# First norm through four PSUM banks, group 0's heads in the prologue, and y rows between weight blocks in a hybrid decoder layer

## What is computed

```python
h = rms_norm(x, norm1_w[layer])
(q, k_c, v_c, k_s, v_s, k_w, v_w, g_nsa, z, xbc, dt_raw,
 gate_a, gate_b) = split_columns(h @ w_in[layer], IN_SIZES)
y_a = nsa_mixer(q, k_c, v_c, k_s, v_s, k_w, v_w, g_nsa, ...)
y_b = ssd_mixer(z, xbc, dt_raw, ...)
merged = jax.nn.sigmoid(gate_a) * (y_a @ w_proj_a[layer]) + jax.nn.sigmoid(gate_b) * (y_b @ w_proj_b[layer])
x = x + merged @ w_out[layer]
x = x + conv_glu_ffn(rms_norm(x, norm2_w[layer]), ffn_w_up[layer], ffn_conv_w[layer], ...)
```

## Time and profile before

| | us |
|---|---|
| three timed runs | 1333.57, 1332.92, 1329.69 (median 1332.92) |
| the profiled execution, whole | 1330.96 |
| its span, first to last instruction | 1329.2 |
| TensorE busy | 1274.7 (96%) |
| VectorE busy | 837.0 (63%) |
| ScalarE busy | 609.5 (46%) |
| DMA, mean rate over the span | 88 GB/s |

### The profile page before, as it was taken

How to read it: one execution, slowest core, us unless ns; L and a number is a source line. 1 busy time by engine, 2 the same in 40 slices (tenths; PEclk the granted TensorE clock), 3 DMA queues, 4 the chain that set the end, 5 groups by cost and what they waited for, 6 DMA issues and landing times.

```text
span 1329.2 us, 18048 instructions
## 1 busy us (share of the span) xinstructions
PE 1274.7 (96%) x6965; PEld 1080.2 (81%) x6965; DVE 837.0 (63%) x1571; ACT 609.5 (46%) x1080; POOL 66.8 (5%) x65
## 2 busy tenths in 40 slices
PE   3998999999999999999999989999999999999999
PEld 2797899879988899877987778887878888888887
DVE  3415788688968797778856443333487878775221
ACT  5524476657665576556664533222432222223110
POOL 1000000400012000400021000000000000000000
PEclk9999999999999999999999999999999999999999
DMA  7312222123221321132212823335223333334231
GB/s 241 102 48 64 64 52 69 41 52 92 57 56 46 98 57 48 41 96 57 64 40 80 284 81 94 95 95 174 64 81 94 95 95 95 95 95 127 95 127 48
DMA packets 185595, 116.37 MB, mean 88 GB/s; under 512 B 25918, under 2 KB 169638, under 8 KB 185510
## 3 DMA queue, kind: packets, MB, share of 16 engines
q1 hardware_dynamic: 182053, 108.92, 28.5%
q10 hardware_dynamic: 3456, 6.29, 1.2%
HBM read 106.80 MB, written 8.39 MB: 87 GB/s over the span
## 4 chain that ended last, share of the span: by engine, by line
PE 78%; DVE 12%; ACT 4%; DMA 2%; issue 2%; SPq 1%; ACTq 1%; DVEq 0%
PE g L556 13%; PE g L557 13%; PE g L558 13%; PE t L549 4%; PE g L589 3%; PE g L591 3%; PE g L590 3%; PE s L809 2%; PE s L714 2%; PE ob L730 2%; DVE w_low L1451 2%; PE s L895 2%; PE s L897 2%; PE s L896 2%; PE t L633 1%
## 5 line engine op out<-in xcount | busy, mean ns | idle before, releaser
L964 ACT ACTIVATE w_high<-wraw 128x1024 fp32r<-128x1024 f32 x175 | 185.1, 1058 | 301.5 <-DMA wraw<-in_ffn_w_up 143.3
L1451 DVE TENSOR_TENSOR w_low<-wraw,w_high 128x1024 fp32r<-128x1024 f32 x175 | 216.7, 1240 | 118.2 <-ACT w_high L964 111.6
L556 PE MATMUL g<-hT_hi,w_high 128*128 128x512 f32 x360 | 161.7, 449 | 5.6 <-DVE hT_lo L1458 3.9
L589 PE MATMUL g<-w_high,hT_hi 128*128 128x256 f32 x512 | 151.4, 296 | 0.0
L591 PE MATMUL g<-w_high,hT_lo 128*128 128x256 f32 x512 | 144.1, 281 | 0.0
L590 PE MATMUL g<-w_low,hT_hi 128*128 128x256 f32 x512 | 144.0, 281 | 0.0
L557 PE MATMUL g<-hT_lo,w_high 128*128 128x512 f32 x360 | 143.2, 398 | 0.0
L558 PE MATMUL g<-hT_hi,w_low 128*128 128x512 f32 x360 | 143.0, 397 | 0.0
L556 PE MATMUL g<-h2T_hi,w_high 128*128 128x512 f32 x352 | 139.9, 397 | 0.5 <-DVE w_low L1451 0.5
L557 PE MATMUL g<-h2T_lo,w_high 128*128 128x512 f32 x352 | 139.5, 396 | 0.0
L558 PE MATMUL g<-h2T_hi,w_low 128*128 128x512 f32 x352 | 139.5, 396 | 0.0
(11 more groups left out here) (319 smaller groups left out, 2515.6 us busy)
## 6 DMA issues: line engine op xcount, KB each, us to landing
wraw<-in_w_in SPq DMA_DIRECT2D x152, 256.0 KB, 3.3
wraw<-in_ffn_w_up SPq DMA_DIRECT2D x88, 256.0 KB, 3.2
wraw<-in_ffn_w_down SPq DMA_DIRECT2D x44, 256.0 KB, 3.1
wraw<-in_w_proj_b SPq DMA_DIRECT2D x32, 256.0 KB, 3.2
yT_lo<-spill SPq DMA_DIRECT2D x6, 1024.0 KB, 8.2
spill<-piece_e ACTq DMA_DIRECT2D x16, 256.0 KB, 3.5
wraw<-in_w_proj_a SPq DMA_DIRECT2D x16, 256.0 KB, 3.1
wraw<-in_w_out SPq DMA_DIRECT2D x16, 256.0 KB, 3.2
```

The costliest lines, as they stand in the source:

```text
L556: nc.tensor.matmul(gb[par][:, :], w, hi, start=k == 0, stop=False)
L589: nc.tensor.matmul(out_, hT[0][:, k, cols], w, start=k == 0, stop=False)
L964: nc.scalar.activation(whi[slot_of(u)][:, :, :], wraw[u % 2][:, :, :], ACT.Copy).then_inc(w_hi, 1)
L1451: V.tensor_tensor(wlo[slot_of(u)][:, :, :], wraw[u % 2][:, :, :], whi[slot_of(u)][:, :, :].bitcast(F32), ALU.subtract).then_inc(w_lo, 1)
```

## The change

Four edits that don't touch what is computed:

1. *Start.* The rows that the first norm needs (slot 2 of `prow`) are loaded from ScalarE's queue, and `pcol` slots 0 and 1 are transposed behind block 0. The root is taken in two pairs; row blocks 0 and 3 are scaled by VectorE, 1 and 2 by ScalarE. x goes through four banks (`s0`, `s1`, `s2`, `ob`) in place of two, first the pieces of row blocks 0 and 1 of four columns, then those of 2 and 3. ScalarE writes `hT_hi` only, and VectorE's difference reads the bank itself. Block 2 is loaded ahead of the compression weights, and SyncE no longer waits for the small loads.
2. *Group 0's heads.* `q_norm` and `k_norm` of group 0 stand ahead of `lo(13)`, their first two transposes at steps 6 and 7 of block 12. `bar[2]` goes. The biases, rounded values and last x evacuation of group 0 move behind block 12 and 13 on ScalarE.
3. *Groups.* SiLU of x ahead of the `pT_hi` of unit 7, SiLU of z right behind the last z evacuation, `qk_root` behind `p_low(7)`, `value_low` behind `ttr(0)` of the group it serves, the transposes of x one step earlier (3, 4, 5, 7 in place of 4, 5, 6, 7), `value_consts(0)` into unit 0.
4. *Gates.* The y transposes at step 7 of block 69 and steps 0 to 2 of block 70; one more gate block ahead of `bar[0]` for every engine; y parts 0 and 1 ahead of block 74's load, 2, 3 and 4 behind the loads of 74 to 76, part 5 between the first two merge blocks; the sigmoids of the early gates spread over three blocks; the merge waits for 2, 4 and 6 y parts in place of 6.

```diff
-            sp.wait_ge(p_loaded, 16 * 16)
+            halves(2, w_in_cols(C_KC + P))
             for q, name in enumerate(("cmp_wk1", "cmp_wv1")):
...
-            y_back(0)
-            for s in range(EARLY_GATES + 4, GATE_BLOCKS):
+            y_rows(0)
+            y_rows(1)
+            for s in range(EARLY_GATES + 5, GATE_BLOCKS):
                 gate_unit(s)
-                y_back(s - EARLY_GATES - 3)
-            y_back(5)
+                y_rows(s - EARLY_GATES - 3)
...
+            def start():
+
+                def columns(k, tiles=range(NT)):
+                    if k >= 4:
+                        pe.wait_ge(h_lo, k - 3)
+                    for i in tiles:
+                        last = nc.tensor.transpose(x1T_banks[k % 4][:, P * i:P * (i + 1)], xt[:, i, P * k:P * (k + 1)],
+                                                   ident[:, :])
+                    if NT - 1 in tiles:
+                        last.then_inc(xT_fill, 1)
+                for tiles in ((0, 1), (2, 3)):
+                    for i in tiles:
+                        pe.wait_ge(xn_ready[i], 1)
+                    for k in range(4):
+                        columns(k, tiles)
...
-            block_of(12)
-            pe.drain().then_inc(bar[2], 1)
+            block_of(12, {6: lambda: backs(0, 0), 7: lambda: backs(1, 0)})
...
+            def h_high(k):
+
+                act.wait_ge(xT_fill, k + 1)
+                nc.scalar.activation(hT[0][:, k, :], x1T_banks[k % 4][:, :], ACT.Copy,
+                                     scale=pcol[:, 2, N1 + k:N1 + k + 1]).then_inc(h_hi, 1)
...
+                    if n == 7:
+                        act.wait_ge(conv_done, g * 6 + 6)
+                        nc.scalar.activation(xcx[:, :, :], xcx[:, :, :], ACT.Silu).then_inc(xc_ready, 1)
...
+                early = {2: chan[:, :, :], 3: xraw[:, :, :], 4: sg[:, 0:2, :]}
+                if s - EARLY_GATES in early:
+                    part = early[s - EARLY_GATES]
+                    nc.scalar.activation(part, part, ACT.Sigmoid).then_inc(gates_ready, 1)
...
+            def h_rest(k):
+
+                dve.wait_ge(h_hi, k + 1)
+                V.scalar_tensor_tensor(hT[1][:, k, :], x1T_banks[k % 4][:, :], pcol[:, 2, N1 + k:N1 + k + 1],
+                                       hT[0][:, k, :].bitcast(F32), ALU.mult, ALU.subtract).then_inc(h_lo, 1)
...
-                    if n == 7 and g < G - 1:
-                        seq.fence()
-                        qk_root(g + 1)
                     lo(u0 + 4 + n)
...
+                if g < G - 1:
+                    seq.fence()
+                    qk_root(g + 1)
                 out_fold(3)
```

More of the change, by code:

```diff
@@ L574, in gemm, with backs @@
                     ins.then_inc(mm_done, 1)
+            def backs(e, g):
+                tau = tau_of(g, K_BACK + e)
+                par = tau % 2
+                pe.wait_ge(tokn_ready, g * 4 + (e + 1))
+                transposes(tau, par, [(tb[par][:, P * i:P * (i + 1)], tokn[e][:, i, :]) for i in range(NT)])
             def half_pair(u, h, between=None):
@@ L617, in _ @@
             pe.wait_ge(const_ready, CONSTS)
-            pe.wait_ge(p_loaded, 16 * 16)
-            transposes(0, 0, [(tb[0][:, P * q:P * (q + 1)], prow[:, q, :]) for q in range(3)])
-            start_of(1, xt, {0: (xn_ready, NT)}, hT)
+            pe.wait_ge(n_loaded, 16 * 5)
+            transposes(0, 0, [(tb[0][:, 0:P], prow[:, 2, :])])
+            start()
             pe.wait_ge(g_rel, 1)
-            transposes(9, 1, [(tb[1][:, P * i:P * (i + 1)], small[:, P * i:P * (i + 1)]) for i in range(NT)])
+            transposes(1, 1, [(tb[1][:, P * i:P * (i + 1)], small[:, P * i:P * (i + 1)]) for i in range(NT)])
             for b in range(2, 5):
@@ L683, in _ @@
                 u0 = U_GRP + GROUP_BLOCKS * g
-                def backs(e, g=g):
-                    tau = tau_of(g, K_BACK + e)
-                    par = tau % 2
-                    pe.wait_ge(tokn_ready, g * 4 + (e + 1))
-                    transposes(tau, par, [(tb[par][:, P * i:P * (i + 1)], tokn[e][:, i, :]) for i in range(NT)])
                 def comp_scores(tiles):
@@ L873, in _ @@
             yb_ = [y[:, 8:24, :] for y in yT]
-            for b in range(1, GATE_BLOCKS - EARLY_GATES):
+            for b in range(2, GATE_BLOCKS - EARLY_GATES):
                 block_of(U_GAT + b)
-            pe.wait_ge(yT_lo, 6)
             for m2 in range(KD // 2):
```

286 lines of the change are left out of this document (138 added, 148 removed).

## The result

The change made the kernel 1.7% faster: 1308.93 us (median of four runs, 1308.11 to 1312.16) against 1331.97 for the kernel before (four runs), a ratio of 0.9831 with a 95% interval of 0.9811 to 0.9851. The forecast was 1307.5 in a range of 1300 to 1316. The total is 1.4 us from the forecast; the terms behind it are not all so close, and two of the five missed by 3.7 and 2.7 us in the profiled execution.

What follows compares the result with a forecast made beforehand. TensorE, busy 96% of the span, was taken as the bound, with 54.5 us idle. Gains of 10.0 + 6.5 + 2.5 + 2.1 + 2.7 = 23.8 us from 1330.96 gave 1307.2, forecast as 1307.5, range 1300 to 1316.

Steps and rivals of the forecast that it cites:

- First steps: Block 0: first transposes of xt near 12, first step about 16.2, steps 0.7 to 1.2 us, end at about 25.
- The start: Up to weight block 3: 10.0 us gained, bounds 4.2 and 12.7, TensorE idling about 2.5 us behind `small`.
- block 3 lands at 31.8: Start: with loads beginning 4.2 us earlier, 5.4 MB at 336 GB/s bring weight block 3 at 31.8 instead of 36.
- End of the prologue: Blocks 12 to 14: no `tokn` wait, first scores at 132.8 against 139.28, 6.5 us gained, bounds 5.0 and 7.2.
- Unit 7: Groups 0 to 2: moving the head roots removes a 0.84 us wait each, 2.5 us gained, bounds 0 and 2.5.
- `value_low`: End of a group: two instructions leave VectorE's row ahead of `combine(3)`, 3 x 0.7 = 2.1 us, bounds 0 and 2.3.
- The gates: Around block 74: a new 3.4 us wait replaces 1.83 + 1.01 + 3.3 = 6.1, 2.7 us gained, bounds -1.0 and 6.4.
- Four banks give nothing: Rival, start: block 0 stays as slow per step, only the loads' 4.2 us gained, 1313; chance 0.12.
- The gates get worse: Rival, gates: early y parts and `yT_lo(0)` hold block 74 back, -1.0 in place of 2.7, 1311; chance 0.12.
- A costly switch: Rival, unit 7: a table load holds ScalarE 1.3 us longer, 2.5 not gained and 3.2 lost, 1313; chance 0.05.
- Loads early enough: Rival: block 3 or block 74 lands 2.5 us sooner, 2.5 to 5 us more gained, 1302.5 to 1305; chance 0.12.
- granted clock of long stretches: Rival: with TensorE busy 98% the clock falls, every per cent costing 13 us, 1348 at 0.97; chance 0.02.

Runs made afterwards that it cites:

- the two kernels with the early load: Changed kernel with weight block 3 loaded behind the first large compression weight: 1307.19 us; the same plus block 74's rounding ahead of y part 0: 1302.81 us.
- the extra switch: Changed kernel with a one-column Exp between SiLU of x and the copies of unit 7 in each group: 1319.33 us.
- the small edits: Changed kernel with `small` ahead of `hi(3)` and `lo(3)` ahead of softplus: 1304.37 us; changed kernel with block 74's rounding ahead of y part 0: 1302.91 us.

## Why the prediction was right, and where it was wrong

- **First steps.** Right: first transposes of xt at 11.3, first step at 16.63 (16.2 forecast). Block 0 ended at 26.7, 1.7 later than forecast: two steps took 2.13 us and one 1.81 where 1.13 is the normal pace; the "1 to 2" that the low clock was to add were 2.7. Steps of under 1.2, as forecast, came only from the fourth on.
- **The start, 10.0 us: measured 6.3, and 7.4 in the mean of seven profiles.** The mechanism stood (a wait behind `small`, on block 3's load), two sizes were off. Block 3 started at 43.9 (39.44 and 19 matmuls of 0.234 more) in place of 40.1. Of these 3.8 us, 2.9 lie ahead of the transposes of `small`, at 36.40 in place of 33.5. The step "block 3 lands at 31.8" had the bytes right: at 218 GB/s from 15 to 20, 377 to 30, then 343 and 217 in the next two microseconds, 5.4 MB had passed by 31.8. But block 4's load, free to go 8.5 us sooner than before, was among them from 30.04 on. That it delayed block 3 is argued from these sizes; no run tested it. The other 0.9 lie behind the transposes: 7.5 us to block 3 where 6.6 were taken. Without the low clock it would have been 6.0; what followed the 3.66 us wait cost 1.5 (transposes 0.76 in place of 0.35, five matmuls 0.43 apart in place of 0.23). The prediction priced a wait of 2.5 and nothing behind it. Its 6.4 us "of the trace" contain, without saying so, that `lo(3)` stands behind softplus and softplus behind block 4's rounding, and that length held (6.3). What it never looked at is that block 4's load then sets when this chain ends: with block 3 early, that alone holds block 3 to 40.2, as the two kernels with the early load show.
- **End of the prologue, 6.5: measured 6.5.** Wait of 0.66 at the third transposes (0.7 forecast), no wait for `tokn`.
- **Unit 7, 2.5: measured 3.4.** SiLU of x ended at 212.1 and the copies started at 212.64 behind 0.52 idle, the "0.5 to spare". The wait was priced by its row's 0.84 and was worth 1.13.
- **`value_low`, 2.1: measured 2.06.**
- **The gates, 2.7: measured 0, and 1.4 in the mean of seven profiles.** The step "a new wait of 3.4 replaces 6.1" held for the wait (3.94). It left out that the clock can fall behind such a wait, though the earlier trace rows showed just that behind 4.43. (It need not: the 3.35 at 770.79 in the kernel before shows that.) With 2.8 for the low clock the sum is 6.7, no less than what it replaced; in the other six profiles the low clock cost 1.4 to 1.6 and the gates gained 1.0 to 2.4. A slip without effect: 0.48 us for four transposes is a quarter of what eight took at 130.60, not half.
- **The total.** 6.3, 6.5, 5.3 and 0, and 0.7 behind the gates, where among others a wait of 0.47 on `w_low` at 980 has gone, make the 18.8 of the two traces, 5.0 short of the forecast 23.8. The first profile was slow at both the start and the gates. With the means of seven, 7.4 and 1.4, the sum is 21.3, and the profiled execution of the kernel before was 1.0 us faster than its median; that makes 22.3 of the 23.0 between the medians. The kernel before has one trace, so how far its own start and gates vary isn't known. The forecast of 1307.5 came within 1.4 us with the start and the gates too high by 2.6 and 1.3 in the mean, and the groups and the rest too low by 1.4: closer than its terms deserve.
- **Rivals.** "Four banks give nothing" came near in its size, not in its mechanism: the start gave 6.3, between its 4.2 and the forecast 10.0, but a step took 1.13 us at the normal pace against 1.6 to 2.0 before, and the wait for `small` swallowed it. "The gates get worse" (-1.0) was nearest in the first profile, with 0; the mean of 1.4 lies between it and the forecast 2.7. "A costly switch" did not come: SiLU of x and the copies kept their places, and the extra switch took 1.30 us in its rows, without a drain. "Loads early enough" didn't come about by itself, and its 1302.5 to 1305 is what the small edits later gave. The granted clock of long stretches stayed at 1.00.

## What to carry to other kernels

A wait that is removed may leave one as long on another queue: for each instruction that waits for a late load, list what stands behind it on its engine, and on the engines that wait for that, before moving a load. Here the order on ScalarE and VectorE was worth 5.2 and 6.7 us at the two places, the order of the loads 2.4 and about 2. A wait of several microseconds on TensorE is to be priced with what can follow it, and a short one with somewhat more than its idle time. A buffer that is freed sooner also starts the next load sooner, beside the one that is waited for. One profile is one execution: here the same code gave marks 4 us apart. And a sum that agrees proves no mechanism: read the rows between.

## What the runs showed of the hardware

- The low clock level behind a wait costs a good part of the wait again. Behind 14 waits of 2.27 to 5.47 us in these kernels, five to nine matmuls of 512 columns were 0.43 us apart, 1.1 to 1.8 us more, and once, behind the 3.94, 14 of them, 2.8 more; where slow transposes came first they added 0.4. Behind five of them (2.27, 2.46, 2.82, 3.16, 4.16) TensorE began at the normal pace and slowed after that. Waits up to 1.85 had nothing of the kind, and neither had the 3.35 in the kernel before, so the length of a wait doesn't settle it.
- At the start the matmuls were 0.43 us apart for two steps while the PEclk column of the stretch from 0 to 33 reads 1.00. There the pace of the matmuls shows the level, and the column doesn't. It differs between executions: of twelve profiles with the changed start, three had their first four steps at 1.13 to 1.14 us.
- A table load is 1.28 us, and the next function starts 0.01 us behind it, with copies and other functions right around it.
